# The first index-query units in quarters: ada_w pieces with homes of their own, scale as columns at once

## The chip, the cores and the metric

One core of a Trainium2 chip runs the kernel. The metric is device time in microseconds for one execution; the times below are a median of three runs and one profiled execution.

## What is computed

Two transformer blocks of different kinds are computed one after the other in float32 on a sequence of 256 rows with 1024 features. Only the head of the first block is touched:

```python
cond = silu(c)
mod = (cond @ ada_w[l] + ada_b[l])[:, None, :]
sh_m, sc_m, g_m, sh_f, sc_f, g_f = split(mod, 6)
h = x * (1.0 + sc_m) + sh_m
z = h @ w_in          # even_mixer: q, k, v, qi, ki, wi, ...
```

ada_w[0] is 1024 x 6144. Its first 1024 columns give the shift sh_m, the next 1024 the scale sc_m: 4 MiB each. Nothing of z can be computed before h, and h needs both.

## The kernel before, in words

**Precision.** Every large product is made of three passes in a reduced float32 form: high times high, high times low, low times high. The scalar engine (ACT) makes the high part of a weight unit (hi_unit, L841 to L849), GpSimd (POOL) the low part (lo_unit, L728 to L733). A unit is 1024 x 256 weights, 1 MiB; units 0 and 1 are the two index-query units G_QI, unit 2 is G_KI (1024 x 192), then the six units of G_QKV[DSA] follow. Two raw, two high and two low buffers alternate; the result of unit g goes to bank 4 + g % 2. hi_unit(g + 2) is called when unit g is evacuated (evac, L896). A raw buffer is loaded again when POOL has made the low part of the unit in it (load_unit, L593).

**Order on each engine.** Each engine runs a list written out by hand; counting semaphores join them. SP issues the loads in order (L632 onward): c, constants, four half blocks of ada_w (512 rows x 512 columns, 1 MiB each) for DVE and four for PE in turn, x before the last pair, units 0 and 1, then half blocks 4 and 5, then the other units with one later half block behind several of them (the table `early`).

**Shift.** The shift columns (blocks 0 and 1) are summed by the vector engine (DVE): modulation_half (L1922) adds four row tiles of a half block, each times a column of cond, into bank 7 and at the end into accg. The 128 partitions of accg are then summed by PE with a column of ones (mod_columns on PE, L1470 to L1486), one product for each 128 columns, which gives a column of modT.

**Scale.** The scale columns (blocks 2 and 3, MOD_PE) are products on PE: mod_half (L1491 to L1497) has cond[:, kt] as the stationary operand, one column wide, and 512 columns of ada_w moving, so a row of 512 results comes out; ACT copies the row to accg (L1043) and mod_columns turns it into columns.

**h.** x is transposed on PE into banks 0 to 3 (transpose_rows, L1468; two of the eight 128-row tiles in each bank, called ht quarter q). When all 16 columns of modT are there (DVE, L1942 and L1943), DVE and ACT share the work: h_full = ht * scale + shift (L1979 on DVE, L866 on ACT), h_hi is a rounded copy (ACT, L873), h_lo the difference (DVE, L2002).

**First products.** first_units (L1409 to L1433) multiplies G_QI[0], with its low weights last, then unit_cols (L1297 to L1324; L1312 and L1313 high, L1321 low, L1287 to L1289 the second half) multiplies G_QI[1], G_KI and the units of G_QKV[DSA]. Behind G_QKV[DSA][0] come the index scores (L1680), whose sums over heads (L2301, L2303), top-k search and mask are DVE's work up to about 99 us; in between DVE sums half block 8.

## Time and profile before

| what | us |
|---|---|
| three runs | 1177.47, 1181.12, 1183.35 |
| median | 1181.12 |
| the profiled execution's own time | 1176.84 |
| its span, first to last instruction | 1175.0 |
| PE busy | 1126.1 (96%) |
| POOL busy | 832.3 (71%) |
| ACT busy | 590.9 (50%) |
| DVE busy | 539.2 (46%) |

The span is the time between the first and the last instruction of the profiled execution. PE busy counts products whose ends are modelled, so products that follow each other overlap in the rows: 0.28 us each, but starts 0.12 us apart. PEld is the loading of stationary operands. A timeline row shows start, length, engine, line, operation, output and inputs, how many instructions were merged, and in brackets the idle time before and what ended it. A windows row shows the stretch, its width, then the busy time and count of PE, PEld, DVE, ACT and POOL (in one for a single line only the engines that it uses), the granted clock of PE (1.00 is 2.4 GHz, 0.50 is 1.2 GHz), the DMA engines' share and GB/s.

### The profile page before, as it was taken

What the parts mean: (1) busy time and instruction counts of PE and PEld (TensorE: products, weight loads), DVE (VectorE), ACT (ScalarE), POOL (GpSimd) and SP (SyncE); (2) the same over time, 40 slices, a digit from 0 to 9 for tenths busy, and PEclk for the clock granted to TensorE, in tenths of its full rate; (3) what the DMA queues carried; (4) which work ended last, traced back from release to release, by engine and by line L of the source; (5) the groups of instructions that cost most, each with busy time, mean ns of one, the idle gap of its engine ahead of it and who ended that gap; (6) DMA issues with size and microseconds to landing.
All of it is one profiled execution on the core that took longest, in us unless ns stands there. A gap on an engine that the chain in (4) does not pass through costs nothing.

```text
span 1175.0 us, 21678 instructions
## 1 busy us (share of the span) xinstructions
PE 1126.1 (96%) x8119; PEld 1030.3 (88%) x8119; DVE 539.2 (46%) x1120; ACT 590.9 (50%) x894; POOL 832.3 (71%) x297
## 2 busy tenths in 40 slices
PE   5899999999999989999999989999999999999997
PEld 2799898999997978899999878999999988999996
DVE  4668877865656675783223441333111333111112
ACT  0455435454543564455545444555776543555444
POOL 3567569988785635888888746556656776988884
PEclk9899989999998999999999999999999999999999
DMA  9987798999985445697656315444444544666652
GB/s 337 320 270 205 249 289 276 337 321 327 308 294 188 133 126 181 188 292 217 195 171 204 108 46 181 133 128 130 139 144 144 190 151 144 204 190 186 189 180 88
DMA packets 253484, 238.03 MB, mean 203 GB/s; under 512 B 18075, under 2 KB 216528, under 8 KB 253424
## 3 DMA queue, kind: packets, MB, share of 16 engines
q1 hardware_dynamic: 235104, 198.70, 54.9%
q10 hardware_dynamic: 17712, 38.28, 9.1%
q8 instruction: 41, 0.67, 0.2%
q0 software_dynamic: 608, 0.22, 0.1%
q14 instruction: 19, 0.16, 0.0%
HBM read 236.12 MB, written 1.05 MB: 202 GB/s over the span
## 4 chain that ended last, share of the span: by engine, by line
PE 71%; DMA 8%; POOL 6%; ACT 6%; DVE 5%; issue 3%; SPq 1%; ACTq 0%; POOLq 0%; DVEq 0%
PE bank L1287 17%; PE bank L1288 17%; PE bank L1289 17%; POOL unit_lo L733 5%; PE bank L1312 3%; PE bank L1321 3%; PE bank L1313 2%; ACT unit_hi L849 2%; DMA raw<-in_ffn_w_up 2%; PE bank L1425 2%; DMA ada<-in_ada_w 1%; PE bank L1528 1%; PE bank L1348 1%; DMA raw<-in_ev_w_in 1%; DVE x L2044 1%
## 5 line engine op out<-in xcount | busy, mean ns | idle before, releaser
L733 POOL TENSOR_TENSOR unit_lo<-raw,unit_hi 128x2048 fp32r<-128x2048 f32 (+5 forms) x87 | 343.7, 3955 | 220.0 <-ACT unit_hi L849 219.2
L1287 PE MATMUL bank<-h_hi,unit_hi 128*128 128x256 f32 x1152 | 327.0, 284 | 0.0
L1288 PE MATMUL bank<-h_lo,unit_hi 128*128 128x256 f32 x1152 | 325.9, 283 | 0.0
L1289 PE MATMUL bank<-h_hi,unit_lo 128*128 128x256 f32 x1152 | 325.9, 283 | 0.0
L784 POOL TENSOR_TENSOR unit_lo<-raw,unit_hi 128x2048 fp32r<-128x2048 f32 (+1 forms) x70 | 257.0, 3672 | 75.1 <-ACT unit_hi L998 65.5
L1287 PEld LDWEIGHTS bank<-h_hi,unit_hi 128*128 128x128 f32 x1152 | 220.7, 192 | 5.3 <-issue 2.5
L1288 PEld LDWEIGHTS bank<-h_lo,unit_hi 128*128 128x128 f32 x1152 | 220.8, 192 | 2.5
L1289 PEld LDWEIGHTS bank<-h_hi,unit_lo 128*128 128x128 f32 x1152 | 220.8, 192 | 0.0
L849 ACT ACTIVATE unit_hi<-raw 128x2048 fp32r<-128x2048 f32 (+5 forms) x97 | 161.3, 1664 | 103.5 <-DMA raw<-in_ffn_w_up 27.3
L787 POOL TENSOR_TENSOR down<-raw_down,down 128x1024 fp32r<-128x1024 f32 x70 | 176.0, 2515 | 0.2 <-ACT down L1024 0.2
L2177 DVE SCALAR_TENSOR_TENSOR work<-bank,cols,work 128x254 f32<-128x254 f32 (+1 forms) x176 | 72.6, 473 | 129.3 <-ACT work L985 129.3
L1287 PE MATMUL bank<-down,y_hi 128*128 128x512 f32 x296 | 116.7, 394 | 3.5 <-DVE y_lo L2209 2.2
L1288 PE MATMUL bank<-down,y_hi 128*128 128x512 f32 x296 | 116.0, 392 | 0.0
L1289 PE MATMUL bank<-down,y_lo 128*128 128x512 f32 x296 | 115.3, 389 | 0.0
L998 ACT ACTIVATE unit_hi<-raw 128x2048 fp32r<-128x2048 f32 (+1 forms) x60 | 90.9, 1514 | 7.0 <-DMA raw<-in_ffn_w_up 6.0
L983 ACT ACTIVATE work<-bank,cols 128x256 f32<-128x256 f32 x44 | 20.8, 473 | 118.1 <-PE bank L1289 101.3
L2206 DVE TENSOR_TENSOR bank<-bank,work 128x256 f32<-128x256 f32 x32 | 13.8, 432 | 133.9 <-ACT work L988 133.9
L1024 ACT ACTIVATE down<-raw_down 128x1024 fp32r<-128x1024 f32 x60 | 63.4, 1056 | 14.4 <-PE bank L1289 14.3
L1312 PE MATMUL bank<-h_hi,unit_hi 128*128 128x256 f32 x272 | 69.7, 293 | 0.0
L1287 PEld LDWEIGHTS bank<-down,y_hi 128*128 128x128 f32 x296 | 55.8, 189 | 14.6 <-issue 4.9
L1313 PE MATMUL bank<-h_lo,unit_hi 128*128 128x256 f32 x272 | 67.8, 286 | 0.0
L1289 PEld LDWEIGHTS bank<-down,y_lo 128*128 128x128 f32 x296 | 55.6, 188 | 12.2
(363 smaller groups left out, 2180.4 us busy)
## 6 DMA issues: line engine op xcount, KB each, us to landing
raw<-in_ffn_w_up SPq DMA_DIRECT2D x86, 512.0 KB, 5.2
raw<-in_w_in SPq DMA_DIRECT2D x60, 512.0 KB, 4.6
raw_down<-in_ffn_w_down SPq DMA_DIRECT2D x44, 512.0 KB, 5.6
ada<-in_ada_w ACTq DMA_DIRECT2D x16, 1024.0 KB, 7.1
raw<-in_w_up SPq DMA_DIRECT2D x64, 256.0 KB, 3.1
raw_down<-in_w_down SPq DMA_DIRECT2D x32, 512.0 KB, 3.5
raw<-in_ev_w_in SPq DMA_DIRECT2D x28, 512.0 KB, 5.3
att<-in_ada_w ACTq DMA_DIRECT2D x14, 1024.0 KB, 8.0
```

Source lines behind the costliest of these rows:

```text
L733: nc.gpsimd.tensor_tensor(ul[g % 2][:, w], raw_home(g)[:, w], uh[g % 2][:, w].bitcast(F32), ALU.subtract).then_inc(lo_up, 1)
L784: nc.gpsimd.tensor_tensor(ul[s][:, 0:w], raw[s][:, 0:w], uh[s][:, 0:w].bitcast(F32), ALU.subtract).then_inc(lo_up, 1)
L787: nc.gpsimd.tensor_tensor(down[:, 1 - k, 1, :], rawd[1 - k][:, :], down[:, 1 - k, 0, :].bitcast(F32), ALU.subtract).then_inc(lo_dn, 1)
L849: nc.scalar.activation(uh[s][:, w], raw_home(g)[:, w], ACT.Copy).then_inc(hi_up, 1)
L998: nc.scalar.activation(uh[s][:, 0:w], raw[s][:, 0:w], ACT.Copy).then_inc(hi_up, 1)
L1024: nc.scalar.activation(down[:, 1 - k, 0, :], rawd[1 - k][:, :], ACT.Copy).then_inc(hi_dn, 1)
L1287: nc.tensor.matmul(o, sh, mh, start=first, stop=False)
L1288: nc.tensor.matmul(o, sh, ml, start=False, stop=False)
L1289: return nc.tensor.matmul(o, sl, mh, start=False, stop=last)
L1312: nc.tensor.matmul(o[:, 0:S], uh[s][:, a], mh[:, kt, :], start=kt == 0, stop=False)
L1313: nc.tensor.matmul(o[:, 0:S], uh[s][:, a], ml[:, kt, :], start=False, stop=False)
L2177: return V.scalar_tensor_tensor(t[:, back:S], bank[4 + s][:, S * j:S * (j + 1) - back], w, t[:, back:S], ALU.mult, ALU.add)
```

## The change

The 8 MiB of shift and scale columns are loaded in quarters of 256 shift and 256 scale columns, each in two row halves: 16 pieces of 512 KB. Every piece has a place of its own in buffers that are not yet in use (shift_home, scale_home), so no load waits for a sum. SP's order is quarter 0, x, quarter 1, unit 0, quarter 2, unit 1, quarter 3, and then the other units. The half blocks that follow in the table `early` each stand behind a later unit than before.

The scale is computed as columns: 128 x 128 of ada_w is the stationary operand and a column of cond moves, 16 such products for each quarter, in two groups of four row tiles for each column (first_scale). DVE sums the shift of a quarter (first_sum), PE makes two columns of it (first_columns), DVE adds them up into modT, scales and shifts the two tiles of that quarter in the bank itself, ACT copies them to h_hi, and DVE subtracts for h_lo (first_rows). PE multiplies both index-query units by the tiles of one quarter before it goes on to the next. G_QI[0] and G_QI[1] are thus finished together. The staged vectors are transposed into bank 7 instead of 6 and earlier in the order.

```diff
@@ loads on SP
+            def load_first(q):
+                for piece in range(2):
+                    for home, c, landed in ((shift_home[q], UC * q, shift_in[q]), (scale_home[q], D + UC * q, scale_in[q])):
+                        sp_.dma_start(home[:, CHUNKW // 2 * piece:CHUNKW // 2 * (piece + 1)].rearrange("p (t n) -> p t n", t=KD // 2),
+                                      W["ada_w"][0][AC * piece:AC * (piece + 1), c:c + UC].rearrange("(t p) n -> p t n", p=P)
+                                      ).then_inc(landed[piece], 16)
...
-            for a in range(MOD_START):
-                load_ada(a)
-                load_mod(a)
-                if a == MOD_START - 2:
-                    sp_.dma_start(x[:, :, :], W["x"][0].rearrange("(t p) n -> p t n", p=P)).then_inc(x_in, 16)
-            for g in range(2):
-                load_unit(g)
-            for a in SUM_FIRST:
-                load_ada(a)
-            early = {G_KI: SUM_EARLY[0], G_QKV[DSA][0]: SUM_EARLY[1], G_QKV[DSA][2]: SUM_IDX, G_QKV[DSA][3]: SUM_ATT[0],
-                     G_QKV[DSA][4]: SUM_ATT[1]}
+            load_first(0)
+            sp_.dma_start(x[:, :, :], W["x"][0].rearrange("(t p) n -> p t n", p=P)).then_inc(x_in, 16)
+            for q in range(1, 4):
+                load_first(q)
+                if q < 3:
+                    load_unit(q - 1)
+            early = {G_KI: SUM_FIRST[0], G_QKV[DSA][0]: SUM_FIRST[1], G_QKV[DSA][1]: SUM_EARLY[0], G_QKV[DSA][2]: SUM_EARLY[1], G_QKV[DSA][3]: SUM_IDX,
+                     G_QKV[DSA][4]: SUM_ATT[0], G_QKV[DSA][5]: SUM_ATT[1]}
@@ ACT
-            for i, j in enumerate(MOD_PE):
-                if i == 1:
-                    hi_unit(0)
-                act.wait_ge(mod_done, 2 * i + 2)
-                nc.scalar.activation(accg[0:1, AC * j:AC * (j + 1)], bank[4 + i][0:1, :], ACT.Copy).then_inc(mod_row, 1)
-            h_high(0, ("modc", 0, 0), modT[:, 0, 8:16], modT[:, 0, 0:8])
-            hi_unit(1)
+            for q in range(4):
+                act.wait_ge(first_ready, q + 1)
+                o = bank[turns["ht", 0, q][0]]
+                nc.scalar.activation(hh[:, 2 * q:2 * q + 2, :], o[:, :].rearrange("p (k t) -> p k t", k=2), ACT.Copy).then_inc(h_hi, 1)
+                for g in range(2) if q == 0 else ():
+                    hi_unit(g)
@@ PE
+            def first_scale(q):
+                o = begin(("first", q))
+                for piece in range(2):
+                    pe.wait_ge(scale_in[q][piece], 16)
+                    for j in range(2):
+                        c = 2 + 2 * piece + j
+                        for kt in range(4 * piece, 4 * piece + 4):
+                            w = slice(UC * kt + P * j, UC * kt + P * j + P)
+                            nc.tensor.matmul(o[:, c:c + 1], scale_home[q][:, w], cond[:, kt:kt + 1],
+                                             start=kt == 4 * piece, stop=kt == 4 * piece + 3)
+            def first_columns(q):
+                o = bank[turns["first", q][0]]
+                pe.wait_ge(ada_acc, q + 1)
+                for j in range(2):
+                    c = UC * q + P * j
+                    mm = nc.tensor.matmul(o[:, j:j + 1], accg[:, c:c + P], ones[:, 0:1], start=True, stop=True)
+                done(mm, ("first", q))
+            def first_highs(q):
+                pe.wait_ge(h_hi, q + 1)
+                for g in G_QI:
+                    if q == 0:
+                        unit_begin(g)
+                    first_part(g, q, uh, hh)
...
-            for half in range(3):
-                mod_half(half)
+            first_scale(0)
+            pe.wait_ge(x_in, 16)
+            transpose_rows(0, x)
             pe.wait_ge(stage_in, 16 * len(STAGED))
+            pe.wait_ge(ada_acc, 1)
...
-            mod_columns(0, (0,), js=[0, 1, 2, 3, 8, 9, 10, 11])
-            mod_half(3)
-            mod_columns(0, (0,), first=False, js=[4, 5, 6, 7, 12, 13, 14, 15])
-            first_units(0, G_QI[:1], low_last=True)
-            unit_cols(G_QI[1], hh, hl)
+            first_columns(0)
+            first_highs(0)
+            for g in G_QI:
+                first_rests(0, g)
+            g0, g1 = G_QI
+            for q, lows in ((1, ((0, g0),)), (2, ((1, g0), (0, g1))), (3, ((2, g0), (1, g1), (2, g1)))):
+                first_scale(q)
+                first_columns(q)
+                for part in lows:
+                    first_lows(*part)
+                first_highs(q)
+                for g in G_QI:
+                    first_rests(q, g)
+            for g in G_QI:
+                first_lows(3, g, True).then_inc(bank_full[4 + g % 2], 1)
@@ DVE
+            def first_sum(q):
+                acc = bank[7][:, 0:UC]
+                for kt in range(KD):
+                    if kt % 4 == 0:
+                        dve.wait_ge(shift_in[q][kt // 4], 16)
...
+            def first_rows(q):
+                o = full(dve, ("first", q))
+                sh, sc = (modT[:, 0, 8 * i + 2 * q:8 * i + 2 * q + 2] for i in range(2))
+                link(V.scalar_tensor_tensor(sc, o[:, 2:4], 1.0, sc, ALU.add, ALU.add))
+                link(V.tensor_tensor(sc, o[:, 4:6], sc, ALU.add))
+                V.tensor_tensor(sh, o[:, 0:2], sh, ALU.add).then_inc(free(("first", q)), 1)
...
+            first_sum(0)
...
+            first_rows(0)
+            for q in range(1, 4):
+                first_sum(q)
+                first_rows(q)
```

first_part(g, q, weight, h) is four products: row tiles 2q and 2q + 1, two column halves each. first_lows waits for the low weights of its unit, first_rests for h_lo of its quarter. In first_rows DVE goes on with two passes over the ht bank (scale and shift), one signal to ACT, a wait for h_hi and two subtractions.

## Rows read from the trace of the kernel before

**Rows 1.** The page: busy time of PE, its granted clock, the DMA share.

```profile
PE 1126.1 (96%) x8119; PEld 1030.3 (88%) x8119; DVE 539.2 (46%) x1120; ACT 590.9 (50%) x894; POOL 832.3 (71%) x297
...
PEclk9899989999998999999999999999999999999999
...
DMA  9987798999985445697656315444444544666652
```

**Rows 2.** Waits of PE, 0 to 60 and 36 to 180 us: total, times, longest.

```profile
PE bank L1497 <- DMA att<-in_ada_w: 8.4, 2, 6.5
...
PE bank L1425 <- ACT h_hi L873: 2.2, 1, 2.2
...
PE bank L1341 <- DVE y_lo L2098: 1.1, 1, 1.1
```

**Rows 3.** Timeline of PE, 0 to 60 us: start, length, line, operation.

```profile
27.75 2.03 PE L1486 MATMUL bank<-consts,accg 128*128 128x1 f32 x16
...
29.98 3.59 PE L1497 MATMUL bank<-accg,cols 128*1 128x512 f32 x8 [0.20 <-DMA accg<-in_ada_w]
...
38.69 3.93 PE L1425 MATMUL bank<-h_hi,unit_hi 128*128 128x256 f32 x16 [2.24 <-ACT h_hi L873]
...
42.42 2.46 PE L1425 MATMUL bank<-h_lo,unit_hi 128*128 128x256 f32 x16
...
44.72 2.08 PE L1425 MATMUL bank<-h_hi,unit_lo 128*128 128x256 f32 x16
...
52.40 0.28 PE L1312 MATMUL bank<-h_hi,unit_hi 128*128 128x256 f32 x1
...
58.16 0.28 PE L1312 MATMUL bank<-h_hi,unit_hi 128*128 128x256 f32 x1
```

**Rows 4.** Windows of the whole core, then of L1486 alone, and the PE timeline.

```profile
36.00:37.00 1.00, 0.45 (x4) 0.36 (x4) 0.45 (x3) 0.11 (x1) 1.00 (x1) 0.74 1.05 387
...
43.00:44.00 1.00, 1.00 (x9) 1.00 (x8) 0.96 (x2) 0.00 (x0) 1.00 (x1) 0.84 0.25 81
...
169.00:170.00 1.00, 1.00 (x10) 1.00 (x9) 0.80 1.07 386
...
170.00:171.00 1.00, 1.00 (x7) 1.00 (x6) 0.50 1.08 401
...
167.27 4.69 PE L1486 MATMUL bank<-consts,accg 128*128 128x1 f32 x32
```

**Rows 5.** Timeline of ACT, 0 to 60 us.

```profile
32.96 1.91 ACT L849 ACTIVATE unit_hi<-raw 128x2048 fp32r<-128x2048 f32 x1 [12.23 <-DMA raw<-in_ev_w_in]
...
46.84 0.60 ACT L898 ACTIVATE h_full<-bank 128x512 f32<-128x512 f32 x1 [4.02 <-PE bank L1425]
...
47.34 1.48 ACT L849 ACTIVATE unit_hi<-raw 128x1536 fp32r<-128x1536 f32 x1
```

**Rows 6.** Timeline of POOL, 0 to 60 us.

```profile
9.27 1.91 POOL L798 DMA_DIRECT2D work<-in_ada_b  x4
...
48.89 3.52 POOL L733 TENSOR_TENSOR unit_lo<-raw,unit_hi 128x1536 fp32r<-128x1536 f32 x1 [1.38 <-ACT unit_hi L849]
```

**Rows 7.** Page, group of L2177, and timeline of DVE to 110 us.

```profile
L2177 DVE SCALAR_TENSOR_TENSOR work<-bank,cols,work 128x254 f32<-128x254 f32 (+1 forms) x176 | 72.6, 473 | 129.3 <-ACT work L985 129.3
...
36.48 0.17 DVE L1942 SCALAR_TENSOR_TENSOR cols<-bank,cols 128x8 f32<-128x8 f32 x1 [5.63 <-PE bank L1486]
...
36.89 1.90 DVE L1979 TENSOR_SCALAR h_full<-bank,cols 128x256 f32<-128x256 f32 x4
...
71.24 0.74 DVE L1919 TENSOR_SCALAR bank<-att,cols 128x512 f32<-128x512 f32 x1
...
107.45 0.17 DVE L2090 RECIPROCAL small<-small 128x2 f32<-128x2 f32 x1 [1.89 <-PE bank L1547]
```

**Rows 8.** Timeline of SP from 55 us.

```profile
61.10 0.51 SPq L630 DMA_DIRECT2D att<-in_ada_w  x1
...
67.35 0.92 SPq L616 DMA_DIRECT2D raw<-in_ev_w_in  x2
```

More of the change, by code:

```diff
@@ L221, in build @@
     ht_turns(0)
+    for q in range(4):
+        turn(("first", q), 6)
     for h in range(HEADS):
@@ L436, in raw_home @@
             return hff if g == FFN_G0[0] else raw[g % 2]
+        shift_home = [ada[0], ada[1], hff, accg[:, D:D + CHUNKW]]
+        scale_home = [ada[2], ada[3], work[:, 1024:1024 + CHUNKW], grow[:, :, :].rearrange("p a n -> p (a n)")]
         def att_count(a, h):
@@ L860, in h_high @@
                 evacuated(act, columns)
-                if n == 0:
-                    def whole(q):
-                        o = full(act, ("ht", n, q))
-                        for kt in (2 * q, 2 * q + 1):
-                            ins = nc.scalar.activation(hf[:, kt, :], o[:, S * (kt % 2):S * (kt % 2 + 1)], ACT.Identity,
-                                                       scale=scale[:, kt:kt + 1], bias=shift[:, kt:kt + 1])
-                        ins.then_inc(free(("ht", n, q)), 1)
-                    def high(q):
-                        evacuated(act, ("ht", n, q))
-                        k = slice(2 * q, 2 * q + 2)
-                        nc.scalar.activation(hh[:, k, :], hf[:, k, :], ACT.Copy).then_inc(h_hi, 1)
-                    whole(1)
-                    high(0)
-                    high(1)
-                    whole(3)
-                    high(2)
-                    high(3)
-                    return
                 for q in range(4):
@@ new lines, in first_columns, with first_part @@
+            def first_columns(q):
[5 more added lines that the diff above has]
+                done(mm, ("first", q))
+            def first_part(g, q, weight, h, last=False):
+                o, s = bank[4 + g % 2], g % 2
+                for kt in (2 * q, 2 * q + 1):
+                    for i in range(2):
+                        a = slice(slot(g) + kt * UC + P * i, slot(g) + kt * UC + P * i + P)
+                        mm = nc.tensor.matmul(o[:, S * i:S * (i + 1)], weight[s][:, a], h[:, kt, :],
+                                              start=kt == 0 and i == 0 and weight is uh and h is hh,
+                                              stop=last and kt == KD - 1 and i == 1)
+                return mm
@@ L1993, in h_columns @@
                     return
-                for q in (0, 2) if n == 0 else (1, 0, 3, 2):
-                    if n and q % 2 == 0:
+                for q in (1, 0, 3, 2):
+                    if q % 2 == 0:
                         dve.wait_ge(h_hi, highs(n, 2 * q + 1))
                     whole(q)
-                for q in range(4) if n == 0 else (3,):
+                for q in (3,):
                     evacuated(dve, ("ht", n, q))
@@ L2274, in _ @@
             evacuated(dve, "cond")
[L2275 to L2276 removed]
+            def first_sum(q):
[3 more added lines that the diff above has]
+                        dve.wait_ge(shift_in[q][kt // 4], 16)
+                    w, dst = shift_home[q][:, UC * kt:UC * (kt + 1)], accg[:, UC * q:UC * (q + 1)] if kt == KD - 1 else acc
+                    if kt == 0:
+                        link(V.tensor_scalar(dst, w, cond[:, 0:1], None, ALU.mult))
+                    elif kt < KD - 1:
+                        link(V.scalar_tensor_tensor(dst, w, cond[:, kt:kt + 1], acc, ALU.mult, ALU.add))
+                    else:
+                        V.scalar_tensor_tensor(dst, w, cond[:, kt:kt + 1], acc, ALU.mult, ALU.add).then_inc(ada_acc, 1)
+            def first_rows(q):
[4 more added lines that the diff above has]
+                V.tensor_tensor(sh, o[:, 0:2], sh, ALU.add).then_inc(free(("first", q)), 1)
+                evacuated(dve, ("first", q))
+                o = full(dve, ("ht", 0, q))
+                for i in range(2):
+                    kt = 2 * q + i
+                    h = o[:, S * i:S * (i + 1)]
+                    ins = V.tensor_scalar(h, h, modT[:, 0, 8 + kt:9 + kt], modT[:, 0, kt:kt + 1], ALU.mult, ALU.add)
+                    if i == 0:
+                        link.mark(ins)
+                ins.then_inc(first_ready, 1)
+                dve.wait_ge(h_hi, q + 1)
+                for i in range(2):
+                    kt = 2 * q + i
+                    ins = V.tensor_tensor(hl[:, kt, :], o[:, S * i:S * (i + 1)], hh[:, kt, :].bitcast(F32), ALU.subtract)
+                    if i == 0:
+                        link.mark(ins)
+                ins.then_inc(free(("ht", 0, q)), 1)
+            first_sum(0)
             o = full(dve, "stage")
```

55 lines of the change are left out of this document (18 added, 37 removed).

## The prediction, made before the change was run

> **What bounds the kernel now.** I read the page first. TensorE (PE) is busy for 96% of the span, and its granted clock is full in nearly every slice [rows 1]. So the kernel is a row of PE instructions, and a change at the head pays or costs one for one if PE is dense behind it. The waits of PE say that it is: from 36 to 180 us it waits twice, 2.2 us and 1.1 us [rows 2]. The head, up to the first product of the index-query units at 38.69, is where PE waits (8.4 us for the ada_w loads alone), and the DMA engines are the reason: their share is 9 tenths and more in the first two slices [rows 1, 2].
>
> The timeline of PE gives the marks I count from [rows 3]. The last half block of ada_w, the ninth MiB of the queue (eight of ada_w, one of x), is multiplied from 29.98. Products start at 38.69; G_QI[1] ends and G_KI starts at 52.40; G_KI ends, and G_QKV[DSA][0] starts, at **58.16**. From there the order of PE's work is the same in both kernels, so the change is worth what it does to 58.16, plus what it does to the vector engine's sums beside it.
>
> **Prices.** A wide product (128x256) costs 0.245 us at the low clock (16 in 3.93) and 0.12 to 0.13 at the full one (16 in 2.08) [rows 3]. A narrow one (128x128 stationary, one column moving, float32) is two instructions of 0.127 us each: 16 in 2.03 [rows 3]. In the longer run at 167.27, 32 take 4.69 us [rows 4]; the clock falls at 169.6 (mean 0.80 in that microsecond), so some 18 ran in 2.3 us and the other 14 in 2.4 us, 0.17 us each at the low clock.
>
> **Removed.** Four half blocks of 8 one-column-stationary products (3.59 us each) with their 16 narrow instructions and 8 of one partition [rows 3], two copies on the scalar engine, and ht evacuations. All of it except what lies between 29.98 and 38.69 was under the loads.
>
> **Added on PE, per quarter.** first_scale: 16 narrow products, 32 instructions: 4.1 us full clock, 5.4 low, 4.7 for the mixed run. first_columns: 4 instructions, 0.5 to 0.7. The wide products of the two units are only cut up: 16 highs and rests per quarter (1.9 or 3.9 us), and 4, 8, 12 and 8 lows.
>
> **The wait that decides.** first_highs(0) goes over both units, and for the second it waits for hi_unit(1), hence for the load of G_QI[1]. That load is queued behind three quarters (6 MiB), x and the first unit: again the ninth MiB. The engines are already saturated [rows 1], so it lands where the ninth MiB lands now, at 30.0. With 1.91 us for the split [rows 5] it is ready at 32.0. Behind this wait on PE stand the scales, columns and products of quarters 1 to 3, although their ada_w pieces have landed or land soon; on the scalar engine, hi_unit(1) stands before the copies of quarters 1 to 3. Everything of quarter 0 ahead of it costs nothing: x transposes, the staged vectors (their last DMA is issued at 11.2 [rows 6]), sum and rows 0 are over well before 30. If that cover went, the first to show would be the staged vectors.
>
> **From 32.0 on.** 4 highs and 8 rests at the low clock: 35.0 (33.5 at the full). Then three quarters in series, because PE runs scale(q+1) only behind rests(q), and highs(q) needs columns(q), the rows on DVE and the copy on ACT:
> - scale and columns 4.7 + 0.6;
> - DVE: three small operations with links, 0.6 us (0.17 each and the step between), two scale-and-shift passes 0.95 (4 take 1.90) [rows 7];
> - ACT: a 128x512 copy, 0.60 [rows 5] and 0.1 to be seen;
> - highs and rests, 16 at 0.245: 3.9.
> The sum is 11.45, so 34.4 for three. The lows before highs(q) fill the 2.3 us in which PE would wait. DVE's sum of a quarter is 8 steps of some 0.5 us (0.47 for one of 256 columns [rows 7]), 4.1 us, and runs beside rests and scale: free, and if PE were faster, it would be next in line. First sums of both units then end at 69.4; 8 more lows, 1.5: T0 = 70.9. The clock rose again at 43.3, in the products that began at 38.69 [rows 3, 4]; the wide products of quarters 2 and 3, with more lows among them, should see a part of that: I take 2.0 off, between 0 and the 10 us that rival B amounts to. T0 = 68.9.
>
> **Behind T0.** Before, the second unit's 5.8 us covered the evacuation of the first and the split of G_KI. Now both units end 1 us apart, and that cover is gone: copy 0.60, G_KI high 1.48, then its low part 3.52 on POOL [rows 5, 6]. G_KI's high is ready at T0 + 1.2, its low at T0 + 4.8; 16 + 8 + 24 products follow with the clock rising: G_KI ends at T0 + 9.2 (8.7 at the full clock). That gives 78.1 against 58.2: **+19.9**.
>
> **The sums.** ada loads on SP are each moved one unit later, and load_ada(4) waits for the third first_sum, with the load of G_QKV[DSA][0] behind it; that load is needed only at T0 + 3. Half block 8 is now issued behind the seventh unit's load, where before it was issued at 61.10, ahead of the load at 67.35 [rows 8]. DVE wants it in the head loop of the index, at 71.24 in the old time; an issue 6 us later makes DVE 3 us late or so, and the top-k chain behind it has 1.9 us of room (DVE waits that long for PE at 107.45) [rows 7]. Half blocks 6 and 7 add up to 1 us. I take +1.5, between 0 and 4.
>
> Sum: +19.9 + 1.5 = **+21.4** on the profiled execution's 1176.8 (span 1175.0), 1198.2. The median of the runs lies 4.3 above that execution, so I name 1202.6.
>
> **Two rules of the skill beside the rows.** The rows show the clock falling at 169.6 while PE is fully busy with narrow products [rows 4]. The Trainium skill (TensorE: Matmul & The Clock Gate, "What's actually happening") has the gate follow how busy PE is. By that rule alone quarters with PE mostly busy would run at the full clock, which is rival B; the row speaks against it, since a busy PE lost its clock.
> The rows also show 0.127 us per narrow instruction. The Trainium skill (same page, "Step-by-step: what each phase is for") has weights loaded ahead beneath running products; by that rule a narrow product would cost next to nothing, which is rival D.
>
> **Rivals.**
> B, the chain as above with the clock full throughout: 33.5, three quarters of 4.1 + 0.5 + 1.6 + 0.7 + 1.9 = 8.8, lows 1.0: T0 = 60.9; G_KI ends at 69.6, +11.4 and no sums: 1188.2, or 1192.5 as a median. For it: the wide products between narrow runs. Against: the fall at 169.6 and the low clock from 36.5 to 43.3 behind narrow products.
> C, low clock throughout and the sums late: 35.0, quarters of 5.4 + 0.7 + 1.6 + 0.7 + 3.9 = 12.3, lows 2.6 (two thirds of it the last 8, the rest lows that outlast DVE in quarter 3): T0 = 74.5; G_KI ends 9.5 later at 84.0, +25.8, sums +4: 1206.6, or 1210.9.
> D, not slower: narrow products cost almost nothing, their weights loading beneath other work. A quarter is then 1.6 + 0.7 + 1.9 = 4.2: T0 = 33.5 + 12.6 + 1.0 = 47.1, G_KI ends at 55.8, -2.4: 1174.4, or 1178.8. It decides from a quarter of 5.0 us, so from 0.02 us for each of the 36 narrow instructions. Against it: 0.127 in a row in which nothing but narrow products stands.
> E, the change does more than its order says: the second unit is not what PE waits for, and the quarters stream beneath the loads, each done as it lands. Quarter 3 ends with the eleventh MiB, which is there at some 36 (nine took 26 us), T0 is about 43, G_KI ends at 52, -6: 1171, or 1175 as a median. The wait on hi_up in first_highs(0) speaks against it, and even without it the narrow products keep PE.
>
> **How the numbers follow.** A 0.58, B 0.20, C 0.13, D 0.06, E 0.03. What a measurement of this kernel can tell from no change is 0.5%, 5.9 us. A, B and C lie beyond it on the slow side: 0.91. D is within it: 0.06. E is faster: 0.03. The range goes from just below B to C, 1190 to 1213; outside are D, E and the far end of C.
>
> **What would show it.** In the profile after: PE waits for ACT unit_hi until about 32 and then works in four bursts some 9 to 12 us apart, each led by 32 narrow instructions; G_KI's products end near 78 instead of 58; the clock is low in the slices from 30 to 70 us; from there on PE has the same rows, 20 us later. I am wrong if narrow instructions take well under 0.1 us, if the second unit's split starts well before 30, or if PE waits after 80 us shrink by what the head lost.

## The result, and the profile after

| | before | after |
|---|---|---|
| median of four runs (of before the three named and one beside after), us | 1179.49 (1177.47 to 1183.35) | 1209.7 (1207.83 to 1213.83) |
| the profiled execution's own time | 1176.84 | 1213.83 |
| its span | 1175.0 | 1212.0 |
| PE busy | 1126.1 | 1147.0 |
| mean granted clock of PE | 0.985 | 0.962 |

The changed kernel is slower: the ratio of the runs is 1.0267, interval 1.0239 to 1.0294, and the medians lie 30.2 us apart. The prediction had 21.4, in a range of 9 to 32 for the difference. Direction and mechanism were right, the size came out almost a third too small.

The page of after, against [rows 1]:

```profile
PE 1147.0 (95%) x8199; PEld 1063.4 (88%) x8199; DVE 546.3 (45%) x1154; ACT 588.5 (49%) x888; POOL 832.3 (69%) x297
...
PEclk8588998999999898999999999999999999999999
...
DMA  9547778999998453767656523444444545665662
```

The second slice (30 to 61 us) has a clock of 5 tenths and DMA at 5: the engines that bound the head before are half idle, and PE runs slowly. The waits of PE from 0 to 90 us, against [rows 2]:

```profile
PE bank L1493 <- ACT unit_hi L852: 14.1, 2, 7.7
```

7.75 us of it is the wait that the prediction put at the root: PE stands in front of the high part of the second unit. The other 6.36 us are the same wait for the first unit; they lie ahead of the second unit's landing and cost nothing beside it. The timeline of PE, against [rows 3]. Behind the second wait come four bursts, and those of quarters 1 to 3 are led by narrow products (L1475); quarter 0's narrow products ran at 7.58, under the loads:

```profile
25.14 1.20 PE L1493 MATMUL bank<-h_hi,unit_hi 128*128 128x256 f32 x4 [6.36 <-ACT unit_hi L852]
34.09 1.22 PE L1493 MATMUL bank<-h_hi,unit_hi 128*128 128x256 f32 x4 [7.75 <-ACT unit_hi L852]
...
36.81 6.82 PE L1475 MATMUL bank<-cols,accg 128*128 128x1 f32 x32
43.49 0.99 PE L1484 MATMUL bank<-consts,accg 128*128 128x1 f32 x4
44.35 1.20 PE L1493 MATMUL bank<-h_hi,unit_lo 128*128 128x256 f32 x4
46.80 2.07 PE L1493 MATMUL bank<-h_hi,unit_hi 128*128 128x256 f32 x8 [1.25 <-ACT h_hi L1024]
...
50.38 6.82 PE L1475 MATMUL bank<-cols,work 128*128 128x1 f32 x32
...
63.17 4.60 PE L1475 MATMUL bank<-cols,gate_rows 128*128 128x1 f32 x32
...
73.65 1.12 PE L1493 MATMUL bank<-h_hi,unit_lo 128*128 128x256 f32 x8
76.35 0.39 PE L1293 MATMUL bank<-h_hi,unit_hi 128*128 128x256 f32 x1 [1.58 <-ACT unit_hi L852]
79.92 1.22 PE L1302 MATMUL bank<-h_hi,unit_lo 128*128 128x256 f32 x8 [1.39 <-POOL unit_lo L736]
```

The low products of the last quarter end at about 74.6 (T0), the key unit G_KI begins at 76.35 (before 52.40) and ends, by the next unit's first row, at 83.85 (before 58.16): +25.7.

Windows of after, all of PE (busy and count, granted clock, DMA share, GB/s):

```profile
24.00:44.00 20.00, 11.11 (x51) 0.50 0.84 262
44.00:48.00 4.00, 2.75 (x12) 0.50 0.00 0
48.00:60.00 12.00, 11.97 (x57) 0.50 0.54 175
```

From 24 to 60 us PE is at the low level, and at 44 to 48 nothing is loaded at all.

Then the sums. The first row is ACT's split of the second unit, against [rows 5]; the next two are DVE's steps of the sums before the index loop, and the last two are PE:

```profile
32.12 1.91 ACT L852 ACTIVATE unit_hi<-raw 128x2048 fp32r<-128x2048 f32 x1 [7.13 <-DMA raw<-in_ev_w_in]
```

```profile
87.83 0.76 DVE L1942 TENSOR_SCALAR bank<-att,cols 128x512 f32<-128x512 f32 x1 [9.89 <-DMA att<-in_ada_w]
96.80 2.34 DVE L1943 SCALAR_TENSOR_TENSOR bank<-ada,cols,bank 128x512 f32<-128x512 f32 x3 [5.84 <-DMA ada<-in_ada_w]
```

```profile
89.70 0.28 PE L1693 MATMUL bank<-consts,work 8*128 8x8 f32 x2
101.57 3.35 PE L1703 MATMUL bank<-att,h_full 64*128 64x128 f32 x16 [4.12 <-DVE work L2363]
```

DVE waits 9.9 us for half block 6 of ada_w and 5.8 for half block 7, starts the sums over heads late, and the second pair of index products waits 4.12 us for it and then runs at half speed (3.35 for 16). Before, PE had the same two steps without a wait:

```profile
64.19 0.28 PE L1670 MATMUL bank<-consts,work 8*128 8x8 f32 x2
...
71.86 1.58 PE L1680 MATMUL bank<-att,h_full 64*128 64x128 f32 x16
```

I use two marks from here on. **Mark 1** is the pair of 8x8 products (64.19 before, 89.70 after: +25.5); **mark 2** is the first product of the sparse scores (96.60 before, 128.81 after: +32.2). The difference stays at +32 to +33 up to the 450th microsecond, and reaches 37 in this pair of profiles, most of it by dips of the clock late in the kernel; over the medians it is 30.2. Single executions of one kernel lay up to 7 us apart (1173.32 to 1180.64 for one of them), so where an experiment ran once I read it by the marks, which don't contain the rest of the kernel. The time stands beside them.

### The profile page after: what moved, and what is told of

Read it like the earlier page. It is cut to its first block, busy times and chain, and to the rows that moved or that the text cites. A ratio compares the mean times of both kernels' runs of the same rounds, so it can differ in the third digit from the quotient of the medians.

```text
span 1212.0 us, 21877 instructions
## 1 busy us (share of the span) xinstructions
PE 1147.0 (95%) x8199; PEld 1063.4 (88%) x8199; DVE 546.3 (45%) x1154; ACT 588.5 (49%) x888; POOL 832.3 (69%) x297
## 3 DMA queue, kind: packets, MB, share of 16 engines
HBM read 236.12 MB, written 1.05 MB: 196 GB/s over the span
## 4 chain that ended last, share of the span: by engine, by line
PE 69%; DMA 7%; DVE 6%; ACT 6%; POOL 6%; issue 3%; SPq 2%; ACTq 0%; DVEq 0%; POOLq 0%
PE bank L1268 16%; PE bank L1269 16%; PE bank L1270 16%; POOL unit_lo L736 5%; ACT unit_hi L852 2%; DMA ada<-in_ada_w 2%; PE bank L1302 2%; PE bank L1293 2%; PE bank L1294 2%; DMA raw<-in_ffn_w_up 2%; PE bank L1475 1%; PE bank L1493 1%; PE bank L1329 1%; SPq L628 1%; DVE x L2067 1%
## 5 line engine op out<-in xcount | busy, mean ns | idle before, releaser
L1268 PE MATMUL bank<-h_hi,unit_hi 128*128 128x256 f32 x1144 | 325.1, 284 | 0.0
L1269 PE MATMUL bank<-h_lo,unit_hi 128*128 128x256 f32 x1144 | 323.9, 283 | 0.0
L1293 PE MATMUL bank<-h_hi,unit_hi 128*128 128x256 f32 x264 | 67.2, 292 | 1.9 <-ACT unit_hi L852 1.9
L1294 PE MATMUL bank<-h_lo,unit_hi 128*128 128x256 f32 x264 | 65.1, 284 | 0.0
```

Source lines behind the costliest of these rows:

```text
L1268: nc.tensor.matmul(o, sh, mh, start=first, stop=False)
L1269: nc.tensor.matmul(o, sh, ml, start=False, stop=False)
L1293: nc.tensor.matmul(o[:, 0:S], uh[s][:, a], mh[:, kt, :], start=kt == 0, stop=False)
L1294: nc.tensor.matmul(o[:, 0:S], uh[s][:, a], ml[:, kt, :], start=False, stop=False)
```

## The experiments

My theory after the result: (a) the order, PE and ACT standing in front of the second unit; (b) the narrow products, priced at the low clock; (c) the sums, by the loads of half blocks 6 and 7 being too late; (d) a term that the prediction lacked, loads in shorter runs (a run is the stretch of a row that is read in one piece). The main rival to (a) and (b) was that three serial round trips between PE, DVE and ACT would cost the same whatever PE did between them.

**1. Both units loaded before quarters 1 to 3.**

```diff
-            for q in range(1, 4):
-                load_first(q)
-                if q < 3:
-                    load_unit(q - 1)
+            for g in range(2):
+                load_unit(g)
+            for q in range(1, 4):
+                load_first(q)
```

> The changed kernel, with both index-query units loaded before quarter 1 instead of behind quarters 1 and 2. In the changed kernel the tensor engine waits 7.75 us for the second unit's high part, starts quarter 1's narrow products at 36.8 and ends G_KI at 83.9. Theory (the second unit's load, the ninth MiB, holds everything): the units are the fourth and fifth MiB, split by 24; quarter 1 starts at about 26.5 as soon as its own pieces have landed; the three quarters take the same 37.8 us; G_KI ends near 73.5, 10 us earlier, and the time falls by 8 to 11 us. Rival (the loads as a whole or the chain behind the quarters set the pace, the wait is only where it shows): G_KI still ends after 80.

Measured: 1204.43 us. Mark 1 at 79.16, 10.5 us earlier than in after. The timeline of PE:

```profile
28.84 6.82 PE L1475 MATMUL bank<-cols,accg 128*128 128x1 f32 x32
...
42.30 3.86 PE L1475 MATMUL bank<-cols,work 128*128 128x1 f32 x32
...
52.67 3.99 PE L1475 MATMUL bank<-cols,gate_rows 128*128 128x1 f32 x32
```

Quarter 1 begins 8.0 us earlier (28.84 against 36.81): the order of loads is worth that much. I had expected quarter 1 at 26.5. The other 2.5 us come from quarter 2, which took 10.37 us in place of 12.79: its narrow products ran at the full clock, 3.86 us in place of 6.82. Quarter 3 gained nothing in all (10.45 against 10.48): its narrow run was shorter, 3.99 for 4.60, its wide products longer. The stall at the index products stays, 4.06 us, so it doesn't hang on the head.

**2. The half blocks of ada_w one unit earlier again.** Half blocks 6 to 10 move one unit up in the table `early`. 8, 9 and 10 then stand where they stood in before; 6 and 7 still stand one unit later than there.

```diff
-            early = {G_KI: SUM_FIRST[0], G_QKV[DSA][0]: SUM_FIRST[1], G_QKV[DSA][1]: SUM_EARLY[0], ...
+            early = {G_KI: SUM_FIRST[:1], G_QKV[DSA][0]: [SUM_FIRST[1], SUM_EARLY[0]], G_QKV[DSA][1]: SUM_EARLY[1:], ...
```

> The changed kernel, with the later half blocks of ada_w put one unit earlier again (half block 6 behind G_QKV 0, 7 behind G_QKV 1, 8 behind G_QKV 2). Theory (the sums come late because their loads stand behind unit loads that wait for GpSimd): the 4.1 us stall of the tensor engine before the second pair of index heads goes, with the low clock behind it; the head up to G_KI's end at 83.9 stays; 5 to 7 us less in all. Rival (the vector engine is late because the head itself is late, whatever the order): the stall stays at 3 us or more.

Measured: 1208.58 us. Mark 1 at 90.41 (+0.7), mark 2 at 124.65 (-4.2), so 4.9 us come back between the two. PE's rows:

```profile
98.89 0.93 PE L1703 MATMUL bank<-att,h_full 64*128 64x128 f32 x8 [0.73 <-DVE work L2363]
100.58 0.93 PE L1703 MATMUL bank<-att,h_full 64*128 64x128 f32 x8 [0.77 <-DVE work L2363]
```

One stall of 4.12 has become two of 0.75, and the products behind it run at full speed. That settles (c): about 5 of the 32 us are the place of these loads in the queue. Five moved together; the two that DVE waited for in after are half blocks 6 and 7.

**3. Without the narrow products.** The scale of quarters 1 to 3 is not computed; all else stays.

```diff
                         for kt in range(4 * piece, 4 * piece + 4):
+                            if q:
+                                continue
                             w = slice(UC * kt + P * j, UC * kt + P * j + P)
```

> The changed kernel without the narrow scale products of quarters 1 to 3 (96 instructions; the scale of these quarters is left out of the result). Theory (they are on the path, at 6.8, 6.8 and 4.6 us): the quarters shrink until the vector engine's sum is next in line, 8.3 us for each of quarters 2 and 3; the units end at about 61 instead of 74.6, G_KI at about 70, 12 to 15 us less. Rival D of the prediction (narrow products cost next to nothing): at most 3 us less. Second rival (nothing else is near the bound): the full 18 us.

Measured: 1199.2 us, mark 1 at 74.42, 15.3 us earlier. PE, in quarters 2 and 3 and at the index products:

```profile
44.98 0.58 PE L1486 MATMUL bank<-consts,accg 128*128 128x1 f32 x4 [1.51 <-DVE accg L2312]
...
52.81 0.98 PE L1486 MATMUL bank<-consts,accg 128*128 128x1 f32 x4 [1.16 <-DVE accg L2312]
...
128.23 1.75 PE L1564 MATMUL bank<-consts,work 128*128 128x128 f32 x6 [2.94 <-DVE work L2117]
```

The narrow runs of the three quarters took 6.82 + 6.82 + 4.60 = 18.2 us; taking them out gains 15.3, because PE now waits 2.7 us for DVE's sum, which the prediction had named as next in line. By the 440th microsecond only 9.8 us are left of the gain. There are two more waits for DVE on the way, 4.3 us (4.1 in after) and 2.9 us (none in after): what is won at the head is partly lost where DVE's own chain of sums and top-k ends last. The rival, that the round trips cost the same in any case, expected almost nothing here and falls; so does the other one on record, the full 18 us.

**4. The narrow products moved into PE's waits.** No work is left out; only PE's list is in another order: the scale of quarter 1 goes ahead of all products of the units, that of quarter 2 ahead of the second unit, and unit 0 is worked on first.

```diff
-            first_highs(0)
-            for g in G_QI:
-                first_rests(0, g)
...
+            first_scale(1)
+            first_columns(1)
+            first_all(0, g0)
+            first_scale(2)
+            first_all(1, g0)
+            first_columns(2)
+            first_all(0, g1, False)
+            first_scale(3)
...
```

> The changed kernel with another order on the tensor engine alone: scale and columns of quarter 1 before any product of the units, those of quarters 2 and 3 between products of earlier quarters, the first unit ended before the second. Theory (a serial chain of narrow products, vector engine, scalar engine and wide products, begun behind the wait): most of the round trips and of the wait are filled; the second unit ends near 65, G_KI near 73, 9 to 12 us less; what is left is the narrow products' own 7 us a quarter. Rival (the tensor engine's work alone fills the time, round trips cost little): under 4 us less.

Measured: 1206.45 us, mark 1 at 76.39, 13.3 us earlier, mark 2 12.1 earlier; the stall for DVE stays (4.13, and 0.77 behind it). PE is filled from 21.8 to 58 us. But see what its products cost:

```profile
21.82 6.99 PE L1475 MATMUL bank<-cols,accg 128*128 128x1 f32 x32 [1.50 <-DVE cols L2332]
...
44.18 6.82 PE L1475 MATMUL bank<-cols,gate_rows 128*128 128x1 f32 x32
```

The run between them, at 32.23, took 6.82 as well. So a PE without waits ran all of them at half speed. Filling the waits was worth 13 us, and more would have been had with the clock.

**5. Experiments 2 and 4 together.**

> Both of the orders that gained: the tensor engine's order with scales ahead, and the half blocks one unit earlier. If the two costs are separate (a serial head, and late sums behind it) they add: the wi transposes come at about 76.4 as with the scales ahead alone, where the changed kernel has 89.7, and the stall before the second pair of index heads falls from 4.1 us to under 2 us, some 17 to 19 us below the changed kernel in all. If the sums are late only because the head is, the stall stays above 3 us.

Measured: 1193.26 us; mark 1 at 73.82 (-15.9), mark 2 at 108.17 (-20.6). Between the two marks it gains 4.8 us on after, as experiment 2 alone did (4.9): the late sums are a cause of their own. Ahead of mark 1 I had expected 76.4, so the head is 2.6 us shorter than in experiment 4. Its first narrow run began 1.2 us earlier (20.59 for 21.82) and took 0.5 less, its second fell into a stretch at full speed (3.96 in place of 6.82), and a wait of 1.98 us for DVE's sum took part of that back. The two experiments alone, both read at mark 2, give 4.2 + 12.1 = 16.3; the rest of the 20.6 is this head, 0.7 by which experiment 2's head ran late, and 1.2 that experiment 4 lost between the marks.

**6. The kernel before, with its loads cut to the run length of the change.** Each half block of shift and scale is loaded in two halves of 256 columns (1 KB for each row in place of 2 KB).

```diff
-                sp_.dma_start(ada[2 + s].rearrange("p (t n) -> p t n", t=KD // 2), half_of(0, MOD_PE[e // 2], s)
-                              ).then_inc(mod_in[s], 16)
+                for i in range(2):
+                    n = slice(UC * i, UC * (i + 1))
+                    sp_.dma_start(ada[2 + s].rearrange("p (t n) -> p t n", t=KD // 2)[:, :, n], half_of(0, MOD_PE[e // 2], s)[:, :, n]
+                                  ).then_inc(mod_in[s], 16)
```

> The kernel before, with its eight first half blocks loaded as two column halves each, so in runs of 1 KB instead of 2 KB. The second unit landed 2 us later than I had put it, and the changed kernel's loads moved 348 GB/s from 16 to 32 us, where the kernel before had 360 to 416. If the run length does it, the DMA rate from 16 to 28 us falls below 360 GB/s here too and the first unit's split starts 1.5 to 2.5 us later than 32.96. Rival (it is the number of DMAs or where the data goes): the rate stays above 370 and the split moves by less than 0.7 us.

Measured: 1179.13 us (before, on the same chip: 1175.48); mark 1 at 67.79, +3.6. The split of the first unit, which starts when its load lands, came at 35.33 against 32.96 [rows 5], +2.4. The windows from 20 to 32 us, first before, then this kernel:

```profile
20.00:24.00 4.00, 2.13 (x6) 1.00 1.04 416
24.00:28.00 4.00, 4.00 (x27) 1.00 1.05 387
28.00:32.00 4.00, 3.80 (x21) 1.00 1.08 360
```

```profile
20.00:24.00 4.00, 1.62 (x5) 1.00 1.08 376
24.00:28.00 4.00, 4.00 (x7) 0.62 1.08 360
28.00:32.00 4.00, 4.00 (x29) 0.95 1.10 348
```

The DMA engines are busy to the same share and move less. The 416 of before and the 376 and 360 of this kernel hold parts of x, which is read in whole rows of 4 KB, and the 360 of before (28 to 32) holds loads of the first unit, which come in 1 KB runs in both. So the clean comparison is 387 (24 to 28, before) against 348 (28 to 32 here). I had expected less than 360 GB/s from 16 to 28; because of x only the window from 16 to 20 shows that (348). In after every window from 16 to 32 us shows 348 or 349 GB/s. That is (d): the ninth MiB lands 2 us later. The edit also doubles the number of transfers, so run length and number aren't told apart.

**7. Dummy products in the wait for the second unit.** Twelve calls of 128x256 on constants stand where PE waits anyway.

```diff
                 for g in G_QI:
                     if q == 0:
+                        if g == G_QI[1]:
+                            keep_warm_early(12, 5)
                         unit_begin(g)
```

> The changed kernel with 12 products of constants (128x256, result unused) put where the tensor engine waits for the second unit. If the low clock is a cost of its own (narrow instructions 0.213 us at the low clock, 0.127 at the full one), the 12 products behind the wait take 1.5 us instead of 2.9, the narrow run of quarter 1 starts at the full clock and takes some 5 us instead of 6.8, and everything after it comes 3 us earlier. If narrow instructions cost 0.213 here for another reason than the clock, only 1.4 us is won.

Measured: 1203.59 us; mark 1 at 85.24, 4.5 us earlier. The rows behind the wait, against those at 34.09 and 36.81 of after:

```profile
34.38 0.74 PE L1498 MATMUL bank<-h_hi,unit_hi 128*128 128x256 f32 x4 [0.61 <-ACT unit_hi L852]
...
35.92 3.63 PE L1480 MATMUL bank<-cols,accg 128*128 128x1 f32 x32
```

The second unit was ready no sooner, and the same narrow run took 3.63 us in place of 6.82; I had expected some 5, and 3 us at the mark. Nothing but the clock differs (1.00 in the window from 36 to 40, 0.50 in after), so a narrow instruction costs 0.113 us at the full clock and 0.213 at the low one. By quarter 2 the clock had fallen again.

**8. Quarters without narrow products.** The scale of a quarter as before, in a row: cond as the stationary column, 256 columns moving, the row copied by ACT and turned by two products of one partition. The quarters and their homes stay, and the half blocks stand as in experiment 5. More than the form changes: the second unit is loaded behind quarter 3, DVE sums quarters 0 and 1 before anything else, and PE and ACT have new orders. First with quarter 3's sum behind quarter 2's rows, then with the sum ahead, the second unit's split ahead of a row copy, and unit 0 finished first.

```diff
+                for kt in range(KD):
+                    if kt % 4 == 0:
+                        pe.wait_ge(scale_in[q][kt // 4], 16)
+                    mm = nc.tensor.matmul(bank[4 if q == 0 else 5][0:1, 0:UC], cond[:, kt:kt + 1],
+                                          scale_home[q][:, UC * kt:UC * (kt + 1)], start=kt == 0, stop=kt == KD - 1)
+                mm.then_inc(mod_done, 1)
```

> The quarters kept, the narrow scale products replaced by the form of the kernel before (one column of cond stationary, 256 columns of ada_w moving, 16 instructions a quarter at 0.213 us and at the full clock), the row copied by the scalar engine; sums of quarters 0 and 1 in front; products of the first unit as soon as quarter and low part are there; the second unit's load last; half blocks one unit earlier. If narrow products and the serial order were the whole loss, the quarters now stream with the loads: the vector engine is next in line (sum and rows of quarters 2 and 3 end near 42), the units end at 45 to 47, G_KI near 54 to 55, against 58.2 in the kernel before: 3 to 5 us faster than that. Rival (a quarter's round trip is too dear in any form): G_KI later than 58.

> The wide scale again (w1_wide_scale), with three moves: the sum of quarter 3 ahead of quarter 2's rows on VectorE, the second unit's high split ahead of the copy of quarter 3's scale row on ScalarE, and the first unit finished before the second one's last quarter. In w1_wide_scale the last high part came at 48.64 because quarter 3's sum only began at 39.88, though its data had long landed, and the key unit began at 53.36 and ended near 60.8 behind GpSimd's low split. Theory (the rest of w1's lateness is order, not work): the sum of quarter 3 ends near 37.6, its high part comes near 43, the last unit's matmuls end near 50, the key unit ends at 56 to 58 against 58.16 before, and the time is 1.5 us less to 1.5 us more than before's. Rival (quarters cost what they cost, 24 narrow or row steps and four round trips between engines): the key unit ends later than 59.5 and the time is over 2 us above before's.

The first form: 1179.15 us (before beside it 1175.48), mark 1 at 66.70, G_KI from 53.36 to 60.85 where I had expected its end at 54 to 55; the rival, a quarter's round trip that is too dear in any form, had it later than 58. The miss: on ACT the split of the second unit stood behind a row copy, which hung on PE's products and those on DVE's sum, and quarter 3's sum began at 39.88 only. The second form, 12 executions against 23 of before: 1176.61 us against 1178.0, ratio 0.9987, interval 0.9974 to 1.0, and mark 1 level with before's 64.19. Mark 2 is not level (100.33 against 96.60). PE:

```profile
36.63 3.61 PE L1493 MATMUL bank<-gate_rows,cols 128*1 128x256 f32 x16
...
54.35 1.22 PE L1322 MATMUL bank<-h_hi,unit_lo 128*128 128x256 f32 x8 [0.85 <-POOL unit_lo L739]
64.14 0.28 PE L1730 MATMUL bank<-consts,work 8*128 8x8 f32 x2
...
73.05 0.93 PE L1740 MATMUL bank<-att,h_full 64*128 64x128 f32 x8 [1.17 <-DVE work L2404]
...
100.33 1.58 PE L1565 MATMUL bank<-att 64*128 64x128 f32 x16
```

The moves gained 2.6 us at mark 1. Time was as expected; the key unit ended at 58.3, 0.3 past the expected stretch, since quarter 3's high part came at 45.76 and not 43: the second unit, loaded last, landed at 38.77, and high(2) and columns(3) stood behind its split. Behind mark 1 it loses 3.7 us, as the first form does (3.8): ACT's split of a later unit waits 3.79 us for its load (0.47 before), the copies of the index products stand behind that split, DVE's sums over heads begin at 71.32 in place of 68.04, and PE waits twice for them. That load was issued 1.2 us earlier than before's (58.91 for 60.13) and landed 3.3 us later; half block 7, issued at 56.55, is still in the queue ahead of it. So the quarters as such cost nothing up to mark 1, and the whole is no faster: 1.4 us over the medians, with an interval that reaches no change. The single profile ends 1.4 us below before's in spite of its later mark 2, at a mean granted clock of 0.989 for 0.985, so the 1.4 can't be put down to the head. The second unit lands at 36 us in before and at 38.8 here, and the two units, their splits and G_KI's low part have to follow it.

**9. Dummy products in the kernel before.** Two behind the fourth row half, four behind the last columns.

```diff
             mod_half(3)
+            keep_warm_early(2, 4)
             mod_columns(0, (0,), first=False, js=[4, 5, 6, 7, 12, 13, 14, 15])
+            keep_warm_early(4, 4)
```

> The kernel before, with two dummy products of 128x256 behind the row half of the fourth load and four behind the last columns, in waits of 0.84 and 2.24 us that TensorE has there anyway; nothing else is changed. Theory (the clock that the units get is set by TensorE's idle time and narrow work just before them): the products that begin at 38.69 run at full clock, their first stretch takes about 2 us less, the key unit ends near 56 in place of 58.16, and the time is 1 to 2.5 us less. Rival (the split of the second unit and its low part set the end of the key unit, and the clock is free): the matmuls are shorter, a wait for ScalarE or GpSimd takes what they save, the key unit ends within 0.5 us of 58.16 and the time is the same within 1 us.

Measured, 12 executions against 23: 1177.98 us against 1178.0, ratio 0.9997, interval 0.9982 to 1.0012. PE:

```profile
38.03 1.19 PE L1430 MATMUL bank<-h_hi,unit_hi 128*128 128x256 f32 x8 [0.32 <-ACT h_hi L873]
39.89 1.27 PE L1430 MATMUL bank<-h_hi,unit_hi 128*128 128x256 f32 x8 [0.67 <-ACT h_hi L873]
...
59.32 1.22 PE L1321 MATMUL bank<-h_hi,unit_lo 128*128 128x256 f32 x8 [0.62 <-POOL unit_lo L733]
63.35 0.28 PE L1677 MATMUL bank<-consts,work 8*128 8x8 f32 x2
```

The first 16 products took 2.5 us in place of 3.93 [rows 3], at full clock, but a wait of 0.67 for ACT stood among them, and one of 0.62 for POOL behind them. The head of this profile began 0.7 us earlier than before's (27.09 against 27.75 for the same columns), so of the 0.84 at mark 1 next to nothing is the edit's. Of the two theories each has a half: the clock does come from what stands just before (G_KI ended at 56.62, 0.9 us earlier when that start is taken off), but the waits for ACT and POOL then take what the matmuls saved, and the time is the same. So the low stretch of the kernel before costs under 1 us net.

**All of them by the marks.** The last column is the difference in time from the kernel before on the same chip; it is one execution against one except for after, the second form of 8, and 9.

| kernel | mark 1 | mark 2 | time against before |
|---|---|---|---|
| before | 64.19 | 96.60 | |
| after | 89.70 | 128.81 | +30.2 |
| 1, both units early | 79.16 | 118.56 | +24.9 |
| 2, half blocks earlier | 90.41 | 124.65 | +29.0 |
| 3, no narrow products | 74.42 | 114.88 | +19.7 |
| 4, narrow products in the waits | 76.39 | 116.75 | +26.9 |
| 5, 2 and 4 together | 73.82 | 108.17 | +17.8 |
| 6, before in 1 KB runs | 67.79 | 100.20 | +3.7 |
| 7, dummy products | 85.24 | 124.40 | +28.1 |
| 8, row form, first and second | 66.70, 64.14 | 100.40, 100.33 | +3.7, -1.4 |
| 9, before with dummies | 63.35 | 95.77 | 0.0 |

Experiments 1, 2 and 4 were expected to give 8 to 11, 5 to 7 and 9 to 12 us of time back. By mark 2 they gave 10.2, 4.2 and 12.1, by the one time of each 5.3, 1.2 and 3.3. Single executions scatter by as much as what is missing, so the runs don't tell whether the gain at the marks reached the end.

## Why the prediction was right, and where its size was off

**Direction, bound and mechanism: right.** PE waits for the second unit until 34.09 and then works in four bursts, three of them led by narrow runs; the clock is low from 24 to 60; behind T0 G_KI takes 9.2 us to the tenth (74.6 to 83.85), with the waits for ACT and POOL that were forecast. Experiments 1, 3 and 4 moved mark 1 by 10.5, 15.3 and 13.3 us when the wait, the narrow products or the serial order were taken out, which neither D nor E allows; B and C have the same chain as A and differ from it in sizes. D fell with the first narrow row: not 0.02 us but 0.213. E fell with the wait at 7.75. B fell with the windows. C, low clock throughout, was nearest in result (1210.9 against 1209.7): its T0 of 74.5 and G_KI end of 84.0 are within 0.2 us of the profile. But its parts are not those of the profile: the clock did rise in quarter 3, and the load was later.

Term by term, forecast and profile:

| term | forecast | measured |
|---|---|---|
| second unit lands | 30.0 | 32.1 |
| highs and rests(0) end | 35.0 | 36.8 |
| quarter 1, scale to next scale | 11.45 | 13.57 |
| quarter 2 | 11.45 | 12.79 |
| quarter 3, to the last lows | 11.45 | 10.48 |
| last 8 lows | 1.5 | 1.0 |
| clock gained back | -2.0 | in the rows above |
| T0 | 68.9 | 74.6 |
| G_KI ends | 78.1 | 83.85 |
| sums | +1.5 | +6.7 |

**Step that was mis-sized, 1: "scale and columns 4.7 + 0.6", behind it "0.17 us each at the low clock".** At the low clock a narrow instruction takes 0.213 us, so scale and columns of quarters 1 and 2 lasted 7.54 us each (36.81 to 44.35) in place of 5.3: +4.5 in all. Quarter 3, half at the full clock, took 5.3. Two things went wrong. The sum took the mixed run (4.7) although the other terms of a quarter stood at the low clock. And the price of 0.127 was the length of a short row divided by its 16 instructions, with the last one's tail in it. From start to start it is 0.109 (32 from 35.92 to 39.41 in experiment 7). At that price the 2.33 us of the run at 167.27 that lie before the fall of the clock hold about 21 instructions and not 18, and the other 11 took 2.36 us: 0.21 each, so the right price stood in that row. The wide price carries a tail too: 16 products at the low clock were 3.93 us as a row, and are 3.58 from start to start (46.80 to 50.38).

**Step 2: "it lands where the ninth MiB lands now".** It counted bytes and took the rate from before. Pieces of 256 columns move at 348 GB/s where 512 columns moved at 387: +2.1, and experiment 6 shows 2.4 on the kernel before.

**Step 3: "+1.5, between 0 and 4" for the sums.** It worked out half block 8, which DVE wants last, and gave "up to 1 us" to half blocks 6 and 7, which come first. Half block 8 held nothing up: its issue did come 6 us later as counted from mark 1 (92.82 against 61.10), but DVE, late itself by then, took it up at 103.03 without a wait for it. DVE's rows show 7 landing at 96.8, and everything behind it, the sums over heads and PE's index products, stood still: +6.7 (25.5 at mark 1, 32.2 at mark 2), of which experiment 2 gave back 4.9. The load of half block 7 is issued at 85.42, behind a unit's load that waits for POOL, and lands 11.4 us after that:

```profile
84.46 0.92 SPq L622 DMA_DIRECT2D raw<-in_ev_w_in  x2
85.42 1.19 SPq L636 DMA_DIRECT2D ada<-in_ada_w  x1
```

When the head is 20 us late, a queue of which each entry waits for the one before keeps every later load that far behind too; I should have followed each of the moved loads to its reader.

**The clock.** The 2.0 us that I took off for it were right by luck: against the forecast price of 3.9 the wide products of quarters 2 and 3 (2.81 and 2.46) came out 2.5 lower, but against what quarter 1 measured at the low clock (3.58) only 1.9. On the rule weighed there (The Trainium skill, TensorE: Matmul & The Clock Gate, "What's actually happening": the gate follows how busy PE is) the runs repeat what the prediction had from one row. L1475 alone in quarter 3, PE busy in full:

```profile
64.00:65.00 1.00, 1.00 (x12) 1.00 (x11) 1.00 0.06 16
65.00:66.00 1.00, 1.00 (x10) 1.00 (x9) 0.80 0.00 0
66.00:67.00 1.00, 1.00 (x7) 1.00 (x6) 0.50 0.72 84
```

By that rule experiment 4, with PE filled, would have had its narrow runs in about 3.6 us each; they took 6.82 and 6.99. The measurement decides: in these rows the clock fell, or was not there, while PE was busy with narrow products. One narrow run behind wide products had it throughout (3.63 us, experiment 7).

**Where the 32 us are.** Of +25.5 at mark 1, 15.3 are narrow products on the path (experiment 3), of which 4.5 by experiment 7's measure is what the low clock does to one run and its neighbours; 8.0 is the second unit's place in the queue (experiment 1); about 2 is the rate of the shorter or more numerous loads. The rest to mark 2 are the sums. These overlap, and I don't claim that they add up to the last microsecond.

## What to carry to other kernels

A wait put into a hand-written list holds back all that is behind it: before a load is moved one place down, follow each engine's list past the instruction that reads it, and follow each load that moves with it to its reader. Turning a product around so that its result comes out as columns costs PE the same at the full clock (3.63 us for a quarter in experiment 7, 3.61 in the row form of experiment 8), and both forms take nearly double at half speed (6.82 and, for the first row of experiment 8's first form, 6.54). What differed is the level they met: the profiles with narrow runs stayed low for most of the head, while the row form had the full clock from 31 us on. The orders differ too, so it isn't shown that the form alone does it. Price an instruction at both levels, from start to start and not by the length of a row, and ask which level its neighbours will run at. And this head, bound by its last load, gained nothing from finer pieces before it: the last piece, its split and the units behind it set the end.

## What the runs showed of the hardware that I had not expected

- A narrow float32 instruction (128x128 stationary, one column moving) takes 0.113 us at 2.4 GHz and 0.213 at 1.2 GHz: 3.63 and 6.82 for 32. It scales with the clock like a wide one (from start to start 0.109 and 0.209, a wide one 0.12 and 0.224).
- The recorded clock is 1.00 at the start of a profile while products run at half speed. In after the window from 8 to 12 us has 1.00 and 20 narrow instructions in 4 us; in before the first eight products of 512 columns took 6.46 us, the next eight 3.60. In experiment 4 this lasts: the record says 1.00 from 20 to 64 us, the narrow runs take 6.8 to 7.0 up to 51, and only the products from 55.22 are fast:

```profile
28.00:32.00 4.00, 4.00 (x19) 1.00 1.10 348
...
55.22 0.63 PE L1493 MATMUL bank<-h_hi,unit_hi 128*128 128x256 f32 x4
```

  So in these profiles the column says nothing up to its first recorded change, and durations must be read in its place. That PE had never left the low speed there is my reading; no record shows it.
- Loads in 1 KB runs moved 348 GB/s at the same busy share (1.10) at which 2 KB runs moved 387 (1.05). Whether the length of the runs or the number of transfers does it is open.
